# Closing part of a mixture-of-experts layer: gate rows and x2 tiles awaited one by one, the second expert's first weights asked for and split later

## What is computed

```python
hf = h.reshape(b * t, d)
top_idx, top_w = route(hf, w_router, router_bias)          # 8 of 64 experts per token
ffn = swiglu(hf, w_sh_gate, w_sh_up, w_sh_down) + routed_experts(hf, top_idx, top_w, w_exp_gate, w_exp_up, w_exp_down)
x = x + g2 * ffn.reshape(b, t, d)
...
y_prompt = rms_norm(yp) * final_gain
```

## Time and profile before

| what | us |
|---|---|
| median of 3 runs (lowest, highest) | 2350.88 (2342.66, 2363.47) |
| the profiled execution's own time | 2358.65 |
| its span, first to last instruction | 2356.5 |
| busy in the span: PE, DVE, ACT, POOL | 2245.4, 1202.4, 962.9, 464.5 |

### The profile page before, as it was taken

One profiled execution on the slowest core, in us unless ns is written; L12 is line 12 of the kernel. 1 busy time (PEld: TensorE's weight loads), 2 busy tenths in 40 slices (PEclk: granted clock), 3 DMA queues, 4 the chain that ended last, 5 costly groups with the idle time before them and its releaser, 6 DMA issues. The chain is left out here.

```text
span 2356.5 us, 43480 instructions
## 1 busy us (share of the span) xinstructions
PE 2245.4 (95%) x12742; PEld 1797.9 (76%) x12743; DVE 1202.4 (51%) x2077; ACT 962.9 (41%) x1722; POOL 464.5 (20%) x525
## 2 busy tenths in 40 slices
PE   6999899999999989999999799999999999999878
PEld 2444567999999989995557688888888878888663
DVE  2423575111223232122557565677777777777756
ACT  2201596121111111111320365666766666667642
POOL 0010000000000000000000234445544444444430
PEclk9999899999999999999999899999999999999999
DMA  9420200111111101115421578889989999899974
GB/s 369 152 112 1 92 2 28 45 45 54 54 45 45 45 9 45 45 36 202 144 69 73 189 230 259 262 260 298 298 282 306 302 294 304 274 300 293 308 232 159
DMA packets 143803, 386.53 MB, mean 164 GB/s; under 512 B 21036, under 2 KB 85364, under 8 KB 116100
## 3 DMA queue, kind: packets, MB, share of 16 engines
q1 hardware_dynamic: 113764, 307.02, 35.7%
q0 software_dynamic: 29808, 78.05, 14.4%
q10 hardware_dynamic: 176, 0.75, 0.1%
HBM read 349.34 MB, written 70.07 MB: 178 GB/s over the span
## 5 line engine op out<-in xcount | busy, mean ns | idle before, releaser
L1981 DVE TENSOR_TENSOR ex_wgu_lo<-ex_stage_gu,ex_wgu_hi (+1 forms) x256 | 296.5, 1220 | 51.0 <-ACT ex_wgu_hi L1907 51.0
L1832 PE MATMUL ex_pgu<-ex_wgu_hi,ex_xT_hi 128*128 (+1 forms) x784 | 315.0, 402 | 7.7 <-DVE ex_xT_lo L1993 7.0
L1765 POOL COPY ex_index_gather<-place_x 128x1 int32 (+1 forms) x101 | 106.9, 1059 | 1047.9 <-issue 1044.5
L1832 PE MATMUL ex_pgu<-ex_wgu_hi,ex_xT_lo 128*128 (+1 forms) x784 | 308.2, 393 | 0.0
L1832 PE MATMUL ex_pgu<-ex_wgu_lo,ex_xT_hi 128*128 (+1 forms) x784 | 307.4, 392 | 0.0
L1907 ACT CAST ex_wgu_hi<-ex_stage_gu (+1 forms) x256 | 249.5, 1047 | 51.5 <-DMA ex_stage_gu<-in_w_exp_up 29.3
L1754 POOL DMA_INDIRECT sum_rows<-ex_y,ex_index_scatter x98 | 174.1, 1776 | 393.9 <-issue 313.2
L906 PE MATMUL cv_ph<-fourth_r,cv_split 128*128 128x272 f32 x1536 | 224.7, 288 | 2.1 <-DVE cv_split L951 2.1
L906 PEld LDWEIGHTS cv_ph<-fourth_r,cv_split 128*128 128x128 f32 x1536 | 204.9, 189 | 2.2 <-DVE cv_split L951 2.2
L432 PE MATMUL qk_pp<-early_late,hT 128*128 128x512 f32 (+1 forms) x432 | 193.7, 602 | 2.3 <-DMA early_late<-in_w_in 2.3
L1832 PEld LDWEIGHTS ex_pgu<-ex_wgu_hi,ex_xT_hi 128*128 128x128 f32 x784 | 148.7, 190 | 39.0 <-issue 9.2
(11 more groups left out here) (317 smaller groups left out, 3922.0 us busy)
## 6 DMA issues: line engine op xcount, KB each, us to landing
ex_stage_gu<-in_w_exp_gate SPq DMA_DIRECT2D x64, 1024.0 KB, 7.1
ex_stage_gu<-in_w_exp_up SPq DMA_DIRECT2D x64, 1024.0 KB, 10.4
ex_stage_dn<-in_w_exp_down SPq DMA_DIRECT2D x64, 1024.0 KB, 7.2
fourth<-in_w_ada SPq DMA_DIRECT2D x24, 1024.0 KB, 8.2
w_ahead<-in_w_in SPq DMA_DIRECT2D x24, 512.0 KB, 3.9
early_late<-in_w_in SPq DMA_DIRECT2D x16, 512.0 KB, 3.9
early_late<-in_w_in SPq DMA_DIRECT2D x3, 2048.0 KB, 16.9
n_work<-in_x_prompt POOLq DMA_DIRECT2D x8, 512.0 KB, 8.1
```

Of the source, the lines that this page charges most:

```text
L1832: last = pe.matmul(pgu[:, :], xT[a][:, k, :], w, start=(k == 0 and (a, c) == PASSES[0]), stop=(k == KT - 1 and (a, c) == PASSES[-1]))
L1981: dve.tensor_tensor(gu_piece(1, slot, q), gu_raw(slot, q), gu_piece(0, slot, q).bitcast(F32), ALU.subtract).then_inc(gu_lo, 1)
```

## The change

In the closing part, `ahead` counts the first four transfers only, and DVE waits for these alone; TensorE waits for each x2 tile by its own semaphore, after the tile's four weight matmuls. SP asks for three x2 tiles at first, for the next two behind TensorE's first and second tile, and for the last three between the requests for the sums. At the start of the stage, SP waits for the first gather to land before it asks for the second expert's gate and up, and ACT and DVE split these behind `hiddens(0)` instead of ahead of `sigmoid(0)` and `silu(0)`.

```diff
+        x2_loaded = [S(f"cb_x2_{t}") for t in range(NT - 1)]
...
                     second = expert(1)
+                    sp.wait_ge(rows_gathered[0], 16)
                     for p in range(2):
                         sp.wait_ge(w_loaded[p], 16)
                         load(p, second, 1)
...
                     sp.wait_ge(gu_lo, NE * NQ4)
-                    for t in range(NT - 1):
-                        put(x2[t], self.x2_rows[t * P:(t + 1) * P, :])
+
+                    def x2_rows(t):
+                        sp.dma_start(x2[t], self.x2_rows[t * P:(t + 1) * P, :]).then_inc(x2_loaded[t], 16)
+
+                    AHEAD = 3
+                    for t in range(AHEAD):
+                        x2_rows(t)
+                    for t in range(AHEAD, AHEAD + 2):
+                        sp.wait_ge(tail_sum, t - AHEAD + 1)
+                        x2_rows(t)
                     sp.wait_ge(all_stored, 1)
                     for t in range(NT):
                         R = rows_of(t)
                         sp.dma_start(sums[t][:R, :], self.sum_rows[t * P:t * P + R, :]).then_inc(sum_loaded[t], 16)
+                        if AHEAD + 2 + t < NT - 1:
+                            x2_rows(AHEAD + 2 + t)
...
+                        cols = [slice(j * 512, (j + 1) * 512) for j in range(2)]
                         for j in range(2):
-                            cols = slice(j * 512, (j + 1) * 512)
                             for f in range(NF):
-                                pe.matmul(psum[t % 4][j][:R, :], a_[:, f, t * P:t * P + R], wd[:, f, cols], start=(f == 0), stop=False)
-                            last = pe.matmul(psum[t % 4][j][:R, :], self.ident[:R, :R], x2[t][:R, cols], start=False, stop=True)
+                                pe.matmul(psum[t % 4][j][:R, :], a_[:, f, t * P:t * P + R], wd[:, f, cols[j]], start=(f == 0), stop=False)
+                        if t < NT - 1:
+                            pe.wait_ge(x2_loaded[t], 16)
+                        for j in range(2):
+                            last = pe.matmul(psum[t % 4][j][:R, :], self.ident[:R, :R], x2[t][:R, cols[j]], start=False, stop=True)
                         last.then_inc(tail_sum, 1)
...
-                    pe.wait_ge(ahead, 16 * (NT + 3))
                     for t in range(NT):
                         last_sums(t)
...
                     split_dn(0, 0)
-                    split_gu(1, 1)
                     sigmoid(0)
                     columns(1)
+                    hiddens(0)
+                    split_gu(1, 1)
                     after = table(act, self.blk_split, 1, NE - 1)
                     with act.If(after >= 1):
                         split_gu(after, after % 2)
-                    hiddens(0)
                     split_dn(1, 1)
...
-                    dve.wait_ge(ahead, 16 * (NT + 3))
+                    dve.wait_ge(ahead, 16 * 4)
```

## The result

The changed kernel takes 2341.1 us (median of 20 runs, 2331.7 to 2350.5) against 2355.8 for the kernel before (20 runs beside it): ratio 0.9945, interval 0.9931 to 0.9960. That is 14.7 us less, 0.6%, and the predicted 2336 is 5.1 us under the measured median: the runs of the kernel before came out at 2355.8 this time, not at 2350.9.

A forecast was written before the change was run, and what follows sets the result against it. The prediction took TensorE to bound the expert loop. Closing -10.0 and start -4.7 made -14.7 us, taking the median from 2350.9 to 2336 us, range 2324 to 2352.

The forecast's parts named there:

- The closing: From the last down matmul to the span's end: shorter waits let DVE's last add end earlier, -10.0 us (7.2 to 10.5).
- wd_prompt beside the last down matmuls: Closing part: DVE waits for four transfers, not twelve, so TensorE starts last_sums(0) 7.5 us earlier.
- full clock in the first tile: Closing part: without TensorE's 7.44 us pause its clock doesn't fall, so the first token tile takes 3.0 us less.
- DVE as the engine that ends last: End of the closing part: DVE's last add at 2338.8, TensorE done at 2338.3, against 2348.78 before.
- the sums held by x2[4]: SP's queue: sums wait behind x2[4], which waits for tail_sum 2 until 2301.4; its 512 KB add some 1.3 us.
- The start: Start of the stage: SP's wait lets the first gather land in 4.5 us instead of 9.2, -4.7 us (0 to -6.3).
- Rival 1: First gather: with even DMA sharing the loads cost it only 1.35 us; start gives 1.4, total 2339.5; chance 0.15.
- The thin cover of the moved split: Split behind hiddens(0): silu(1) 1.25 us late, but the gates that read it still covered; costs nothing, at most 0.8 us.
- The carry: Expert loop of some 950 us: TensorE carries it, so a shift at its start should arrive at its end.
- Rival 4: Expert loop: TensorE's late stalls swallow the 4.7 us earlier start, only the closing counts, total 2341; chance 0.14.
- Rival 2: Closing part: sums or an x2 tile hold DVE and TensorE, closing gives only 4, total some 2342; chance 0.08.
- rival 3: Expert loop: each of 97 scatters lands 0.3 us later, loop grows by 29 us, total 2365; chance 0.08.

The follow-up runs named there:

- experiment 1: Changed kernel with the start of the stage put back as before (no SP wait, early split), closing part kept: ratio 0.9957 to the kernel before.
- experiment 3: Changed kernel with the second expert's split put back early, SP's wait kept: 47.2 us from the stage before's last matmul group to block 2's sigmoid.
- experiment 4: Changed kernel without SP's wait for the first gather, later split kept: 43.6 us from the stage before's last matmul group to block 2's sigmoid.
- experiment 8: Changed kernel with 14 throwaway matmuls before the first rows: 44.3 us from the stage before's last matmul group to block 2's sigmoid, closing 57.2.
- experiment 10: Changed kernel with 60 throwaway matmuls on TensorE before the first rows: ratio 1.0134 to the kernel before.
- experiment 2: Kernel before with only the two edits at the start (SP's wait and the later split): ratio 0.9984 to the kernel before.
- experiment 5: Changed kernel with all eight x2 tiles asked for at once instead of spaced: 57.05 us from the last down matmul to the span's end.
- experiment 6: Kernel before with 16 throwaway matmuls in TensorE's pause before last_sums(0): first token tile 5.15 us, last down matmul to span's end 68.9 us.
- Run 9: Changed kernel with 5 throwaway matmuls before the first rows and x2[4] asked for behind the first sum: ratio 0.9930 to the kernel before.

## Why the prediction was right

*The total, -14.7 predicted and measured.* That the two agree to a tenth is luck. The six runs with the changed closing part as it is (the changed kernel, experiments 1, 3, 4, 8 and 10) took 56.0 to 57.2 us for it, against 65.8 in the two with the old one (before, experiment 2): a gain of 8.5 to 9.9. The start interval was 39.5 to 39.7 in the three runs with the changed start and nothing added to it (the changed kernel, experiments 2 and 5), 43.6 to 44.4 in the three with the old one (before, experiments 1 and 6): a gain of 3.9 to 5.0. The parts are what was confirmed.

*The closing, -10.0 predicted, -9.8 measured.* Its parts held: wd_prompt beside the last down matmuls and the first tile without a pause (7.6 us earlier, 7.5 predicted); full clock in the first tile (3.0 us; shown by experiment 6); no wait for an x2 tile; then DVE as the engine that ends last, its last add 48.3 us behind the last down matmul where the prediction has 2338.8 - 2290.75 = 48.05. One step was right in size and wrong in reason. The prediction has the sums held by x2[4], 11.25 us behind the last down matmul; they went out at 11.52, and what came last was the final scatter, which started at 8.69 and needs 2.8. Run 9 shows it: without tail_sum 2 ahead of them the sums went out at 11.56 all the same. What x2[4] cost was its place just ahead of the first sum: 5.3 us from the sum's request to its use, 3.6 in run 9, so 1.7 where the prediction has 1.3. With it gone the closing was 1.2 us shorter.

*The start, -4.7 predicted, -4.6 measured.* The gather was taken at 4.5 us and takes 4.6; the 4.5 was chosen between an estimate of 4.2 and a nearest row of 4.9, so that the size fits so well is luck too. Rival 1, even shares between the gather and SP's loads, falls as to the time: taking the loads away gave back 4.6 us, not 1.4, and putting them back (experiment 4) took it again. But the prediction's argument against it, long turns of the loads, isn't what the trace shows. Once the gather moves, its packets and the loads' alternate nearly one for one, and that stretch costs 1.7 us, near the rival's price. The rest is the 2.9 us by which its first packet comes later, which neither had. The thin cover of the moved split held, with silu(1) 1.1 us late against 1.25 predicted and nobody waiting. The prediction costed the move at nothing and said that it belonged to the wait, without saying what the wait alone would do: it loses 7.7 us of start interval against the changed kernel, of which 2.7 are a fall of the clock that the prediction did not see.

*The carry.* Rival 4 falls by experiment 10 for a delay of 44 us; that a start 4.9 us earlier arrives too is argued from it. The claim needed it: in the profiles of the twelve kernels, all with the same loop, it took 928 to 947 us from the sigmoid of block 2 to the last down matmul. A shift of 4.9 us can't be seen in one run against that, nor did experiment 2's ratio show it. What makes the loop vary by 19 us was not tried.

*Rival 2 and rival 3.* The closing gave 9.8: no tile held it up, and the sums cost the 1.2 us that run 9 gave back, not the 6 of rival 2. Rival 3, later scatters for 97 blocks, isn't seen: the loop took 964.2 before and 964.0 after. With the loop's spread of 19 us that is no proof that the phase has no effect, only that it had none as large as the 29 us of the rival.

## What to carry to other kernels

A transfer on which the next stage's first instruction waits should be alone on the DMA engines: what is asked for beside it and needed later can wait for its semaphore. But whoever consumes the later transfer must move back with it, or an engine stands in front of a semaphore with urgent work queued behind. And one semaphore for a dozen transfers makes everybody wait for the last of them; count by who needs what.

## What the runs showed of the hardware

- A gather of 128 rows that took 9.2 us beside two loads of 1 MB takes 4.6 without them, more than its share of the bytes would say (1.4 us). The larger part is a late start: its first packet moved 4.8 us after the gather's start in the four runs with the loads beside it (before, experiments 1, 4 and 6) and about 2 us after it in the eight others. In the kernel before, 1319.5 is also when the first of the two loads lands, 4.8 us after its issue; whether the gather waits for that, no run shows. The Trainium skill, "DMA: Bandwidth & Descriptors", section on queues, rings and completion order, says that a DMA engine changes between queues only at a packet's end. The 86 packets of the gather's queue against 81 of the loads' from 1319.5 to 1322.0 agree with taking turns; the late first packet isn't explained by it.
- TensorE's granted clock fell in a pause of 5.74 us (experiment 3: 0.50 from 1330 to 1335, the 1.2 GHz level) and stayed up in the one of 1.51 before the last down matmuls (1.00 from 2276 to 2288 in the changed kernel). A fall cost 2.4 to 3.0 us here each time (run 9, experiments 3 and 6). Throwaway matmuls in the pause keep the clock up (experiment 6: 1.00 throughout) or take the slow stretch in place of the real work (run 9), if they are done before the real work comes.
